# Four gathered rows of u get places of their own, and the remaining picks are spread over 160 rows instead of 128

## What is computed

```python
def peer_ffn(h, w_pq, peer_keys, peer_u, peer_v):
    q = jnp.einsum("bsd,dhk->bshk", h, w_pq).reshape(B, S, PEER_HEADS, 2, KEY_DIM)
    sub = jnp.einsum("bshpk,hpnk->bshpn", q, peer_keys).astype(jnp.float32)
    s, i = lax.top_k(sub, PEER_TOPK)
    ...
    top_s, pos = lax.top_k(cand, PEER_TOPK)
    idx = jnp.take_along_axis(cidx, pos, axis=-1)
    gate = jax.nn.softmax(top_s, axis=-1).astype(h.dtype)
    ...
        u = jnp.take(peer_u, i_blk, axis=0)
        a = jax.nn.gelu(jnp.einsum("td,thkd->thk", x_blk, u)) * g_blk
        v = jnp.take(peer_v, i_blk, axis=0)
        return jnp.einsum("thk,thkd->td", a, v)
```

## Time and profile before

| what | value |
|---|---|
| median of 3 runs | 3032.91 us (3031.19 to 3035.19) |
| profiled execution, span | 3035.1 us |
| first dot to last dot on DVE | 1864.42 to 2507.83 us |
| DVE busy, share of the span | 71% |
| POOL: indirect DMAs of rows (L2133) | 256, 476.4 us |
| DVE: dots (L2570) | 217, 493.8 us, mean 2291 ns |
| bytes moved by DMA in the span | 805.40 MB |

### The profile page before, as it was taken

How to read it: one execution, slowest core, us unless ns; L and a number is a source line. 1 busy time by engine, 2 the same in 40 slices (tenths; PEclk the granted TensorE clock), 3 DMA queues, 4 the chain that set the end, 5 groups by cost and what they waited for, 6 DMA issues and landing times.

```text
span 3035.1 us, 36610 instructions
## 1 busy us (share of the span) xinstructions
PE 2628.2 (87%) x13062; PEld 2228.3 (73%) x13062; DVE 2165.0 (71%) x3282; ACT 1420.4 (47%) x2695; POOL 839.1 (28%) x563
## 2 busy tenths in 40 slices
PE   8999999999999999999999997877434007999997
PEld 6787878888888878888778897877433006888886
DVE  5996465454545565566445568999999988998987
ACT  5466454343434454545554443322299915333333
POOL 0000000010100000000000003666688865675653
PEclk9999999999999999999999999999755558999999
DMA  9544555555555546556435567999999997999997
GB/s 255 185 149 153 181 183 190 194 181 195 187 190 189 193 160 222 180 161 218 149 118 176 189 225 277 419 418 419 410 420 421 420 411 232 408 408 408 408 407 303
DMA packets 278956, 805.40 MB, mean 265 GB/s; under 512 B 33161, under 2 KB 73329, under 8 KB 245008
## 3 DMA queue, kind: packets, MB, share of 16 engines
q1 hardware_dynamic: 221216, 417.26, 40.9%
q0 software_dynamic: 57344, 385.91, 31.4%
q10 hardware_dynamic: 240, 0.18, 0.0%
HBM read 799.09 MB, written 4.19 MB: 265 GB/s over the span
## 4 chain that ended last, share of the span: by engine, by line
PE 36%; DMA 8%; POOL 7%; issue 5%; DVE 4%; ACT 1%; DVEq 0%; POOLq 0%; ACTq 0%
PE ps L2677 7%; POOL expert_rows L2133 7%; PE ps L222 6%; PE ps L224 6%; PE ps L223 6%; DMA expert_rows<-in_peer_u,index 5%; PE ps L2684 2%; PE ps L2686 2%; PE ps L2685 2%; DMA expert_slabs<-in_peer_v 1%; DVE junk L2570 1%; DMA expert_pieces<-in_peer_v,piece_index 1%; PE ps L2669 1%; PE ps L2219 1%; PE ps L2217 1%
## 5 line engine op out<-in xcount | busy, mean ns | idle before, releaser
L207 DVE TENSOR_TENSOR wl<-ring,wh 128x1024 fp32r<-128x1024 f32 (+2 forms) x616 | 732.0, 1229 | 631.6 <-ACT wh L195 629.0
L195 ACT CAST wh<-ring 128x1024 fp32r<-128x1024 f32 (+2 forms) x612 | 605.7, 1040 | 632.1 <-PE ps L224 567.7
L2133 POOL DMA_INDIRECT expert_rows<-in_peer_u,index x256 | 476.4, 1861 | 589.6 <-DVE wl L207 429.6
L222 PE MATMUL ps<-wh,th 128*128 128x512 f32 (+1 forms) x1464 | 576.7, 394 | 6.5 <-DVE wl L207 4.5
L223 PE MATMUL ps<-wl,th 128*128 128x512 f32 (+1 forms) x1464 | 568.0, 388 | 0.0
L224 PE MATMUL ps<-wh,tl 128*128 128x512 f32 (+1 forms) x1464 | 568.0, 388 | 0.0
L2570 DVE CUSTOM_DVE_ANT_0 junk<-expert_rows,h 128x2048 f32<-128x2048 f32 x217 | 493.8, 2291 | 38.1 <-DMA expert_rows<-in_peer_u,index 36.4
L222 PEld LDWEIGHTS ps<-wh,th 128*128 128x128 f32 x1464 | 275.8, 188 | 67.0 <-DVE wl L207 6.8
L224 PEld LDWEIGHTS ps<-wh,tl 128*128 128x128 f32 x1464 | 275.6, 188 | 57.0
L223 PEld LDWEIGHTS ps<-wl,th 128*128 128x128 f32 x1464 | 275.9, 188 | 54.3
L2609 DVE SCALAR_TENSOR_TENSOR x_and_pieces<-expert_pieces,const,x_and_pieces 128x896 f32<-128x896 f32 x256 | 288.4, 1148 | 24.2 <-DMA expert_pieces<-in_peer_v,piece_index 12.1
(11 more groups left out here) (412 smaller groups left out, 4498.0 us busy)
## 6 DMA issues: line engine op xcount, KB each, us to landing
ring<-in_w_in SPq DMA_DIRECT2D x80, 1024.0 KB, 5.1
expert_slabs<-in_peer_v SPq DMA_DIRECT2D x128, 576.0 KB
ring<-in_w_up SPq DMA_DIRECT2D x64, 1024.0 KB, 5.1
ring<-in_w_down SPq DMA_DIRECT2D x64, 1024.0 KB, 5.0
ring<-in_w_in SPq DMA_DIRECT2D x68, 512.0 KB, 5.0
ring<-in_w_out SPq DMA_DIRECT2D x32, 1024.0 KB, 5.0
ring<-in_w_peer_q SPq DMA_DIRECT2D x16, 1024.0 KB, 5.1
ring<-in_w_ukv SPq DMA_DIRECT2D x8, 1024.0 KB, 5.6
```

Of the source, the lines that this page charges most:

```text
L195: self.nc.scalar.copy(self.wh[:, i % 2, two, 0:w], self.ring[:, i, two, 0:w]).then_inc(self.high_ready, 1)
L207: self.nc.vector.tensor_tensor(self.wl[:, i % 2, two, 0:w], self.ring[:, i, two, 0:w], self.wh[:, i % 2, two, 0:w].bitcast(F32), ALU.subtr ...
L222: mm(o, hi, wh, start=start and k == 0, stop=False)
L2133: nc.gpsimd.indirect_dma_start(p.rows[:, n % GR, :], None, peer_u, bass.IndirectOffsetOnAxis(ap=p.index[:, n:n + 1], axis=0)).then_inc(p.l ...
```

## The change

Rows 0 to 3 get places of their own (`early_rows`): one where keys once lay, two in the memory of x, one where the gains of the norm lay. All of these are free once `h2` is made, x has been written out and unit 0 is picked, and POOL issues these four first, before it waits for the memory of the ring. The eight places then take rows 4 to 11 at the points where rows 0 to 7 stood, and row n goes to place (n - 4) % 8; row n + 8 still waits for row n to be read, now from row 12 on. `PICK_DOTS` is 160 instead of 128. Since the last rows come to lie in other places, the slabs of `peer_v`, `x_and_pieces` and `expert_pieces` change places, and the counts that SyncE waits for follow.

```diff
-PICK_DOTS = 128
+PICK_DOTS = 160
+EARLY_ROWS = 4
...
+def row_place(p, n):
+
+    return p.early_rows[n] if n < EARLY_ROWS else p.rows[:, (n - EARLY_ROWS) % GR, :]
+
+
+def row_landed(p, n):
+
+    k = n - EARLY_ROWS
+    return (p.early_landed[n], 16) if k < 0 else (p.landed[k % GR], k // GR * 16 + 16)
...
         def _(pool):
+            pool.wait_ge(h2_ready, NH)
+            pool.wait_ge(x_kept, 16)
             pool.wait_ge(p.picked, 1)
-            for n in range(GR):
-                if n < RING:
-                    pool.wait_ge(core.low_ready, (base + 7) * (2 * RING) + (2 * n + 2))
+            for n in range(EARLY_ROWS):
+                gather_row(nc, p, n, peer_u)
+            for i in range(GR):
+                if i < RING:
+                    pool.wait_ge(core.low_ready, (base + 7) * (2 * RING) + (2 * i + 2))
                 else:
-                    pool.wait_ge(core.slabs_used, (base + 7) * RING + (RING + 1 + n % 2))
-                gather_row(nc, p, n, peer_u)
+                    pool.wait_ge(core.slabs_used, (base + 7) * RING + (RING + 1 + i % 2))
+                gather_row(nc, p, EARLY_ROWS + i, peer_u)
...
-        slabs = place("expert_slabs", [P, SLOTS, SUMMED], at=-112 * KB)
-        summed = place("x_and_pieces", [P, NH, PIECE], at=-85 * KB)
-        pieces = place("expert_pieces", [P, GR, PIECE], at=-78 * KB)
+        slabs = place("expert_slabs", [P, SLOTS, SUMMED], at=-77 * KB)
+        summed = place("x_and_pieces", [P, NH, PIECE], at=-84 * KB)
+        pieces = place("expert_pieces", [P, GR, PIECE], at=-112 * KB)
...
             for m in range(SLOTS):
-                sp.wait_ge(freed, NH * PICKS + (4 * SUMMED * (m + 1) - 1) // (4 * D) + 1)
+                sp.wait_ge(freed, NH * PICKS + (3 * KB + 4 * SUMMED * (m + 1) - 1) // (4 * D) + 1)
                 sp.dma_start(slabs[:, m], v_rows[:, m, PIECE:D]).then_inc(slab_in[m], 16)
-            sp.wait_ge(freed, NH * PICKS + 5)
+            sp.wait_ge(freed, NH * PICKS + GR)
             sp.wait_ge(p.x_kept, 16)
             sp.dma_start(summed[:], rows_out[:, :, 0:PIECE]).then_inc(sums_in, 16)
...
-            for n in range(GR, UNITS * TOPK):
+            for n in range(EARLY_ROWS + GR, UNITS * TOPK):
                 if n % TOPK == 0:
                     pool.wait_ge(p.picked, n // TOPK + 1)
                 pool.wait_ge(*row_read(n - GR))
                 gather_row(nc, p, n, peer_u)
```

More of the change, by code:

```diff
@@ L2127 @@
 PE_LAG = 7
+def row_place(p, n):
[3 more added lines that the diff above has]
+    return (p.early_landed[n], 16) if k < 0 else (p.landed[k % GR], k // GR * 16 + 16)
 def gather_row(nc, p, n, peer_u):
     nc.gpsimd.indirect_dma_start(
-        p.rows[:, n % GR, :], None, peer_u, bass.IndirectOffsetOnAxis(ap=p.index[:, n:n + 1], axis=0)
-    ).then_inc(p.landed[n % GR], 16)
+        row_place(p, n), None, peer_u, bass.IndirectOffsetOnAxis(ap=p.index[:, n:n + 1], axis=0)
+    ).then_inc(row_landed(p, n)[0], 16)
 def out_and_queries_stage(core, block, w_out, w_queries, gain_rows, keys_in_dram, x_home, peer_u, p, z, z_th, z_tl):
@@ L2167, in out_and_queries_stage @@
         p.landed = core.new(*[f"row_landed{i}" for i in range(GR)])
+        p.early_landed = core.new(*[f"early_row_landed{i}" for i in range(EARLY_ROWS)])
         p.scores_out = scores_out
@@ L2431, in peer_stage @@
         piece_landed = core.new(*[f"piece_landed{i}" for i in range(GR)])
-        landed, rows = p.landed, p.rows
         place = core.place
@@ L2565, in dot @@
             def dot(n):
-                dve.wait_ge(landed[n % GR], n // GR * 16 + 16)
+                dve.wait_ge(*row_landed(p, n))
                 k = by_order.index(n)
@@ L2569, in dot @@
                     dve.wait_ge(freed, k + GR - 1)
-                nc.vector.tensor_tensor_reduce(out=junk[:, k % 2, :], in0=rows[:, n % GR, :], in1=p.h2[:, n // PICKS, :],
+                nc.vector.tensor_tensor_reduce(out=junk[:, k % 2, :], in0=row_place(p, n), in1=p.h2[:, n // PICKS, :],
                                                scale=1.0, scalar=0.0, op0=ALU.mult, op1=ALU.add,
@@ L2704, in dot_by_tensor @@
             def dot_by_tensor(i, n):
-                pe.wait_ge(landed[n % GR], n // GR * 16 + 16)
-                turn_row(rows[:, n % GR, :], 4 * i + 4)
+                pe.wait_ge(*row_landed(p, n))
+                turn_row(row_place(p, n), 4 * i + 4)
                 if i >= 2:
@@ L2986, in build @@
         p.rows = place("expert_rows", [P, GR, D], at=-112 * KB)
+        in_x = place("early_rows_in_x", [P, NH, D], at=-48 * KB)
+        p.early_rows = (place("early_row_by_keys", [P, D], at=-16 * KB)[:], in_x[:, 0, :], in_x[:, 1, :],
+                        place("early_row_in_gains", [P, D], at=80 * KB)[:])
         p.best = place("best", [P, 2, TOPK], at=32 * KB)
```

## The result

The changed kernel took 3043.62 us (median of five, 3039.32 to 3047.77), the kernel before 3033.78 us (3031.19 to 3035.19) beside it: a ratio of 1.0029, with an interval from 1.0018 to 1.0040, or 8.8 us slower (5.5 to 12.1). The forecast was 5.0 us. The same two kernels once more, on the chip of the first experiments, gave 1.0017 (1.0008 to 1.0026), 5.2 us slower (2.4 to 7.9).

The account below looks back on a forecast made before the run. The prediction took the stretch of gathers to be bound by DMA bytes until row 255 lands. Late landing +4.3 (start's 2.0 off), thinner queue +1.5 and tail -0.8 gave +5.0 us, 3037.9 us, range 3031.0 to 3043.5.

Parts of the forecast that it names:

- What bounds the stretch: From 1880 us gathers are bound by bytes until row 255 lands; a microsecond there is a microsecond of the total.
- Early rows, 2.0 us kept of 10.0: Four early rows could save 10.0 us; row 13 still waits for row 5's dot, so the start is 2.0 us earlier.
- Picks, the lag: Rows 119 to 159 need 120.8 us on DVE; at row 160 it lags 18.3 us, against 7.5 at worst before.
- Picks, what the lag costs: Row 168 lands 4.3 us later, the start's 2.0 taken off; 1.5 us more from DMA's drop; nothing gives it back.
- thinning: At row 168's dot, a lag of 8.2 us lets DMA drop for 10 us: 1.5 us more, bounds 0 to 3.
- The tail, 0.8 us: At the end, x_and_pieces loads after the last dot, freeing DMA but delaying the first add: 0.8 us earlier.
- The sum: Whole kernel: +4.3 + 1.5 - 0.8 = +5.0 us, median 3037.9 us.
- my own case: The forecast's main case for the total: +2 to +8 us, 3035 to 3041 us; chance 0.55.
- The early rows carry through: Rival: DMA never runs dry behind row 12, the start keeps all 10.0 us; 3030 or 3021 us; chance 0.10.
- The two parts cancel: Rival: the start keeps 4.9 us and row 168's late landing takes 5.1 us; about 3032 us; chance 0.20.
- The queue thins more: Rival: queue runs low behind every part after row 131; landing costs 7.3, thinning 3; +10.3, 3043 us; chance 0.15.

Follow-up runs that it names:

- picks160: The kernel before with PICK_DOTS = 160 and nothing else: 3047.84 us, a ratio of 1.0028 to the kernel before.
- early128: The changed kernel with PICK_DOTS = 128 again, so early rows and moved places without late picks: 3040.48 us, 0.9998 of the kernel before.
- late_sums: The kernel before with only the load of x_and_pieces waiting for the last dot, as in the changed kernel: 3038.69 us, 0.9995 of the kernel before.
- ring12_160: The changed kernel with a ring of twelve places up to row 107, eight after, PICK_DOTS still 160: 3039.21 us, 0.9991 of the kernel before.
- ring12_128: The changed kernel with a ring of twelve places up to row 107 and PICK_DOTS = 128: 3029.34 us, 0.9955 of the kernel before.
- after_again: The changed kernel unchanged, measured once more as a control on another chip: 3046.20 us, 1.0017 of the kernel before.
- ring12_again: The changed kernel with twelve places up to row 107 and PICK_DOTS = 128, measured once more on another chip: 3030.83 us, 0.9966 of the kernel before.
- picks144: The kernel before with PICK_DOTS = 144 alone: 3045.12 us, 1.0011 of the kernel before.

## Why the prediction was right, and where it was off

**What bounds the stretch.** Held. The time of row 255 gave the sign of the median in every kernel that moved it by more than the table's spread, and more than half of the size.

**Early rows, 2.0 us kept of 10.0.** Held as a mechanism; the size was too large, and what is kept can't be told from nothing. At row 110, where DVE waits for the row in all of these kernels and so marks its landing, the changed kernel is 1.4 us ahead of the kernel before and 0.9 ahead of picks160, which has its picks; at rows 26 and 35, the first for which DVE waits, it is 0.1 ahead of picks160. early128 is 1.7 us behind the kernel before and 0.3 behind late_sums. The spread is 1.4 us. Row 13 was to be issued at 1879.0, and it was issued at 1881.29, which is 1879.04 and the profile's shift of 2.25. The drop of DMA was there (0.34, 111 GB/s). That "nothing in the change moves" the dot of row 5 is shown from the other side by ring12_160 and ring12_128, where row 13 no longer waits for it and 10.1 us (against picks160) and 8.3 us come through.

**Picks, the lag.** The sum of steps was right to the tenth: 120.8 us from row 119 to row 160, measured 2279.69 - 2158.84 = 120.85. Behind row 119 DVE first waited for a row again at row 192 (191 in after_again and picks160), forecast about 195. DMA moved 369 GB/s from 2210 to 2300.

**Picks, what the lag costs.** Row 168 was to land 4.3 us later with the start's 2.0 taken off, so 6.3 without, and thinning to add 1.5: 7.8 us gross. picks160, which has no early rows, is 8.1 us behind at row 192. I had written that nothing gives the delay back. That step failed by a little: from row 192 to row 255 picks160 regains 2.8 us, the changed kernel 2.5 and 1.2 in after_again. Between 1.0 and 1.3 us of it lie in the last distance, from row 254 to row 255, which is 5.22 us in the kernel before. In its last 23 us ahead of dot 255 the kernel before moves 362 GB/s, picks160 413:

```profile
2485.00:2508.00 23.00, 0.00 (x0) 0.00 (x0) 14.15 (x15) 0.00 (x0) 1.07 (x1) 0.50 0.95 362
```

My first reading stopped at 2485 us and took the gathers to be bound by bytes right to row 255. What thins DMA in those last rows of the kernel before the runs leave open: not `x_and_pieces` alone, since the last row is as late in late_sums, and not the early end of the picks, since with `PICK_DOTS` at 119 the last row comes as soon as with 160.

By row 248 the sum for the changed kernel was 4.3 + 1.5 = 5.8 us, measured 6.4 and, in after_again, 7.9. (The 2512 us that the prediction named for row 255 does not follow from this sum, which gives 2507.8 + 5.8 = 2513.6; the dot started at 2515.08, 2512.8 without the shift of 2.25.)

**The tail, 0.8 us.** Not shown and not refuted: -1.5 us with an interval of 4.3 faster to 1.2 slower in late_sums. Both sides of my estimate were visible as mechanisms, the first addition 1.5 us later, the cover of DMA at the last rows better, but the second came from another cause than the load I gave it to.

**The sum.** +5.0 us forecast, 5.2 and 8.8 measured. The first comparison's interval (5.5 to 12.1) lies just above the forecast, the second's (2.4 to 7.9) around it. The median of 3043.62 us stands 0.1 beyond the upper end of the range (3031.0 to 3043.5), beside a kernel before that was itself 0.9 us slower than when the forecast was made; by the ratio the changed kernel would be at 3032.91 x 1.0029 = 3041.7 us, within it, and 8.8 us is a little more than the +2 to +8 of my own case. At row 255 the terms ahead of the tail gave +5.8, the profiles have 5.0 and 6.8. That the first is just the forecast total is in part luck: the start kept less than the 2.0 us taken off, and the regain of 1.2 to 2.5 us behind row 192, which I had excluded, made up for it. The medians of kernels with picks at 160 lie 3 to 5 us above what row 255 says in three of four comparisons (8.8 to 5.0, 8.5 to 5.3, and 9.9 to 4.9 for ring12_160 against ring12_128) and 1.6 below in after_again (5.2 to 6.8); ring12_128 gains some 5 us more in the median than at row 255 (13.7 to 8.5) and once about as much (10.3 to 9.8). Most of this goes with where the profiled execution lay among its own runs: 2.6 and 2.3 us below the median in the changed kernel and picks160, 2.1 above in after_again, 4.0 above in ring12_128 and 0.8 above in ring12_again. Only for ring12_160 (3.2 above) against ring12_128 it explains little. So it need be no further cost of the late picks. One profile each, with 3 us of spread in the rest column, can't exclude that something behind row 255 adds to it.

**The rivals.** *The early rows carry through* fell: it wanted row 13 issued by about 1874, and DMA to stay full behind row 12, where it moved 111 GB/s. *The two parts cancel* fell with the 8.1 us at row 192. *The queue thins more* is nearer than I gave it credit for in the first median (3043 us forecast, 3043.6 measured), but not by its mechanism: its price at row 168 and behind it was 7.3 + 3 = 10.3 with the start taken off, and the profiles have 6.4 to 7.9 at row 248.

## What to carry to other kernels

A load that starts earlier ahead of a ring gains only if the first reuse of a place comes earlier too: ask which row waits for which, and when that one is read (four early rows with eight places kept at most 1.4 us of 10, no more than the spread, with twelve places 8.3 to 10.1). Work that moves from a stretch where an engine has room into one where it has 0.29 us a row to spare should be summed in steps until the lag stands beside what the ring's places bear; here a lag of 7.5 us cost 1.5 and one of 18 us cost 8. And count from a common event ahead of the change, since two profiles of the same code stood up to 5.5 us apart before the stretch began (1864.4 and 1869.9).

## What the runs showed of the hardware

DMA engines can be "busy" and short of work: in the stretch of the late picks their share is 0.97 to 0.98 at 372 to 375 GB/s, in picks144 0.98 at 390, and 1.01 at 420 when enough rows are queued. The share alone hid a loss of 11%; the bytes showed it. Deeper holes (0.34 at 111 GB/s) show in both.

An indirect gather takes POOL 0.94 us to issue, and longer when it begins while a dot runs on DVE: then the issue ends 0.8 us after that dot. In the kernel before 181 of the 256 issues take 1.8 us or more. Every one of them began during a dot, and every one ended 0.79 to 0.84 us after the end of that dot. Of the 72 issues that took less than 1.3 us, 70 began while no dot ran, many of them beside a part of the picking. Row 13 is an example: its issue begins at 1879.04, 0.36 us into the dot that started at 1878.68 and ends at 1880.97, and it ends at 1881.79. So the 2.75 us in the prediction is not the price of following a dot but of meeting the next one near its start; an issue that begins later in a dot takes 1.91. The Trainium skill's page "SBUF — State Buffer" (section on the two separate sides) says that some of VectorE's instructions can lock GpSimd out of the port that they share, and that the one that starts first holds it for its whole instruction. The trace agrees with that order of events. Whether a dot is such an instruction, and whether it is this port that holds the issue back, no run here shows.

The last rows arrive every 3.9 us instead of 2.50 once the slabs of `peer_v` load beside them: in the changed kernel rows 251 to 255 are dotted 3.95, 3.92, 3.93 and 3.95 us apart, while DMA moves 417 GB/s from 2485 to 2515 us.
